# Start of the first feed-forward stage, place of the hidden low part, unrolled layers, half-block splits and rounded expert passes in a two-part transformer kernel

## The chip, the cores and the metric

The kernel runs as one program on one core of a Trainium2 chip. A core has five engines that each work through a queue of their own: TensorE (PE, matrix products; PEld is its weight load), VectorE (DVE), ScalarE (ACT), GpSimd (POOL) and SyncE (SP). They wait for each other through semaphores. The metric is the device time in microseconds (us); the profile shows one execution.

## What is computed

256 tokens of width 1024 pass two layers and then a hybrid layer with a mixture of experts:

```python
for l in range(DEPTH):                       # 2 layers
    mod = silu(c) @ w_ada[l] + b_ada[l]      # 9 rows of 1024: shift, scale, gate of three stages
    x = x + 0.5 * g1 * swiglu(modulate(x, sh1, sc1), ffn1_gate, ffn1_up, ffn1_down)   # 2816 wide
    x = x + g2 * token_mix(modulate(x, sh2, sc2), ...)                                # attention and merge
    x = x + 0.5 * g3 * swiglu(modulate(x, sh3, sc3), ffn2_gate, ffn2_up, ffn2_down)
x = rms_norm(x) * final_norm
x = x + gate1 * mix(modulate_2(x, ...))      # convolution and forgetting attention
h2 = modulate_2(x, ...)
x = x + gate2 * sum over experts e of comb[e] * swiglu_e(h2)    # 32 experts in 4 groups, width 256
```

All is float32. `comb` picks for each token one group of eight experts by softmax of `h2 @ w_rg + b_rg`, and in it the two best experts by `h2 @ w_re + b_re`.

## The kernel before

**Split products.** A float32 product is made of three products in the rounded type fp32r: each factor is split into a high part (the value rounded, by a copy on ScalarE) and a low part (the value less the high part, by a subtraction on VectorE), and `mm3` (L1542 to L1546) adds hi*hi, lo*hi and hi*lo in PSUM. A product with plain float32 operands is possible too and is used for small things: transposes with `ident`, the gathering of tokens, the spreading of results.

**The weight stream.** The weights come as units of 6144 columns (128 rows), each of three blocks of 2048 columns (1 MB). SP loads a block into one of three places of `raw` (`load_stream`), ScalarE makes `w_hi` (`split`, L466; L473 in the experts), VectorE makes `w_lo` (L854, L860), and TensorE waits for the block in `need`. Semaphores: `landed` for a load, `hi_done` and `split_done` count blocks, `used[j]` says that TensorE is through with block j of a unit. A feed-forward unit is 256 of the 2816 hidden columns: blocks 0 and 1 hold gate and up weights (k-chunks 0 to 3 and 4 to 7 of 512 columns), block 2 the down weights. An expert is one unit.

**Modulation.** `w_ada` comes in pairs of two columns of 128 values (1 MB a pair). VectorE multiplies each with silu(c) and sums (`ada_pair`, L877; `first_pair`, L1118), two instructions of 1024 columns a pair. POOL loads pairs into two slots of `ada_w` beside the layers (L441), each when `ada_done` says that the slot's former pair is used. The eight pairs of the very first shift and scale come ahead, loaded by SP into five places (`first_w`).

**A norm.** ScalarE sums squares (L482), VectorE scales (`norm_tile`, L898), TensorE turns the tokens (`norm`, L1581), both engines apply shift and scale (L499, L907) into `uTf`, ScalarE rounds it to `uT_hi` (L505), VectorE makes `uT_lo` (L912). TensorE keeps itself busy with zero products meanwhile (`keep_warm`, L1534).

**The start.** SP asks for c, pairs 0 and 1, x, all constants, the vectors, then pairs 2 to 7 with the blocks of unit 0 between them. VectorE does pairs 0 to 3 with the splits of blocks 0 and 1 between, pair 4, the norm of tile 0, pairs 5 to 7, the modulation (two instructions over all columns), and inside the layer loop the norm of tile 1. Then `gate_up` of unit 0 runs, all k of tile 0 first, then of tile 1.

**A feed-forward stage** (`ffn`, four times). In each pass of its loop TensorE turns the hidden values of unit i-1 (`turn`, L1610), does `gate_up(i)` and then `down(i-1)`. ScalarE does silu (L517, L519), VectorE `hidden` (L920), ScalarE the high part of the turned values (L523), VectorE the low part (`h_split`, L924). On VectorE the first unit has this order: split of block 0 of unit 1, pair 0 of the gate, `hidden(0)`, splits of block 1 of unit 1 and block 2 of unit 0, pairs 1 to 3 of the gate, the gate itself (L891, L893). Then the loop over i begins: `h_split(i-1)`, a pair (in ffn1), split of block 0 of unit i+1, a second pair (in ffn1), `hidden(i)`, split of block 1 of unit i+1, split of block 2 of unit i. In ffn2 a pass has one pair, from i = 2 on. Loops over i and the loop over the two layers are hardware loops (`Fori`) on PE, ACT, DVE and POOL.

**Routing.** After the last norm (`norm(n6 + 1, n6 + 2)`) TensorE makes the logits (48 products of 36 columns) in PSUM, VectorE adds the bias (L1409), ranks groups and experts, and makes `pick`, a 0/1 matrix for each of four groups that says which token stands at which of its 128 places (L1440). TensorE gathers the tokens of a group by plain float32 products with `pick` (`gather`, L2012: 16 products of 128 columns a group). Order on TensorE: gather 0, turned picks (L2020), gather 1, expert weights (L2026), gate/up of expert 0, gathers 2 and 3, and on. An expert is 24 products for gate and up and 12 for down, in 128 columns of places. After a group ScalarE copies the result (L798) and `spread` (L2066) puts it back to the tokens by four plain float32 products of 512 columns.

## Time and profile before

| | us |
|---|---|
| median of 3 runs | 2011.21 |
| lowest and highest run | 2007.62, 2019.69 |
| the profiled execution | 2009.42 |
| its span, first to last instruction | 2007.8 |

| engine | busy us | share of the span |
|---|---|---|
| PE | 1840.3 | 92% |
| PEld | 1492.2 | 74% |
| DVE | 1350.6 | 67% |
| ACT | 924.7 | 46% |
| POOL | 46.9 | 2% |

The mean granted TensorE clock was 0.940 of full. The stages follow each other: start to 58 us, ffn1 to 256, attention and merge to 496, ffn2 to 715, layer 1 the same to 1399, hybrid layer to 1664, routing to 1698, experts to 1985, end. A row of the timeline gives an instruction's start and length, and in square brackets how long the engine stood idle before it and which instruction released it. "issue" as releaser means that the engine waited for nothing that the profile shows. A group's busy time says nothing of whether it lies on the path; the idle times of TensorE do. A plain float32 product has two records in a count (x8 is four products).

### The profile page before, as it was taken

Reading aid. Unit: us, or ns where it says so; the run is one execution under the profiler, and the core shown is the slowest. Engines: PE = TensorE matmul, PEld = TensorE weight load, DVE = VectorE, ACT = ScalarE, POOL = GpSimd, SP = SyncE. Lnnn points to the kernel's source line nnn. Section 1 sums busy time; section 2 is a strip of 40 time slices with the busy share of each in tenths; the row PEclk is TensorE's granted clock in tenths of the full one; section 3 lists DMA queues with packets and bytes.
Section 4 is the critical chain, followed back from the end, with each engine's and each line's share of the span. In section 5 each row is a group of like instructions: output and inputs, shape, how many; then the busy total and the mean of one; then the engine's idle time right before and its main releaser. Section 6 shows DMA issues by size and latency. Waiting matters only on the chain.

```text
span 2007.8 us, 25016 instructions
## 1 busy us (share of the span) xinstructions
PE 1840.3 (92%) x8870; PEld 1492.2 (74%) x8870; DVE 1350.6 (67%) x1773; ACT 924.7 (46%) x1122; POOL 46.9 (2%) x92
## 2 busy tenths in 40 slices
PE   3799999999799988999999988998997998999997
PEld 2688777787588857886788767886876677878875
DVE  6777755856666557776557566665677275988885
ACT  2344453654444343444436552444433234777664
POOL 0000000000000000000000000000000000000000
PEclk6899998999899989999989998999999597999999
DMA  9788731324666648884412346665586051899993
GB/s 383 262 314 311 290 135 58 113 96 149 228 238 248 247 151 329 309 310 170 155 64 87 124 153 245 250 251 199 209 307 238 0 176 58 334 343 371 345 342 124
DMA packets 61361, 437.52 MB, mean 218 GB/s; under 512 B 6752, under 2 KB 7136, under 8 KB 9056
## 3 DMA queue, kind: packets, MB, share of 16 engines
q1 hardware_dynamic: 47056, 339.29, 45.6%
q0 software_dynamic: 12672, 92.28, 12.3%
q10 hardware_dynamic: 1552, 4.89, 0.7%
q8 instruction: 49, 0.80, 0.2%
q14 instruction: 32, 0.26, 0.0%
HBM read 435.38 MB, written 1.05 MB: 217 GB/s over the span
## 4 chain that ended last, share of the span: by engine, by line
PE 77%; DVE 12%; issue 4%; ACT 4%; DMA 3%; SPq 0%; DVEq 0%; ACTq 0%; POOL 0%; POOLq 0%
PE bank L1544 22%; PE bank L1545 21%; PE bank L1546 21%; DVE w_lo L854 3%; DMA ada_w<-ada_pairs 2%; DVE ada_w L877 2%; PE bank L1739 2%; ACT w_hi L466 1%; PE bank L1756 1%; DMA raw<-weight_stream 1%; PE bank L1610 1%; PE bank L1717 1%; PE bank L1713 1%; PE bank L1719 1%; PE bank L1534 1%
## 5 line engine op out<-in xcount | busy, mean ns | idle before, releaser
L854 DVE TENSOR_TENSOR w_lo<-raw,w_hi 128x2048 fp32r<-128x2048 f32 x214 | 489.5, 2291 | 330.9 <-ACT w_hi L466 330.5
L466 ACT ACTIVATE w_hi<-raw 128x2048 fp32r<-128x2048 f32 x214 | 408.7, 1913 | 462.9 <-PE bank L1546 462.9
L1544 PE MATMUL bank<-w_hi,uT_hi 128*128 128x512 f32 (+3 forms) x1456 | 564.3, 388 | 17.2 <-DVE w_lo L854 6.1
L1545 PE MATMUL bank<-w_lo,uT_hi 128*128 128x512 f32 (+3 forms) x1456 | 551.2, 379 | 0.0
L1546 PE MATMUL bank<-w_hi,uT_lo 128*128 128x512 f32 (+3 forms) x1456 | 549.6, 378 | 0.0
L1544 PE MATMUL bank<-w_hi,r_arena 128*128 128x512 f32 (+1 forms) x744 | 305.8, 411 | 36.6 <-DVE r_arena L924 31.6
L1544 PEld LDWEIGHTS bank<-w_hi,uT_hi 128*128 128x128 f32 x1456 | 278.3, 191 | 74.9 <-issue 12.7
L1546 PEld LDWEIGHTS bank<-w_hi,uT_lo 128*128 128x128 f32 x1456 | 277.8, 191 | 51.3
L1545 PEld LDWEIGHTS bank<-w_lo,uT_hi 128*128 128x128 f32 x1456 | 278.2, 191 | 47.9 <-issue 1.4
L1545 PE MATMUL bank<-w_lo,r_arena 128*128 128x512 f32 (+1 forms) x744 | 300.3, 404 | 0.0
L1546 PE MATMUL bank<-w_hi,r_arena 128*128 128x512 f32 (+1 forms) x744 | 297.9, 400 | 0.0
L877 DVE CUSTOM_DVE_ANT_0 ada_w<-ada_w,cmpw 128x1024 f32<-128x1024 f32 x176 | 207.2, 1220 | 30.4 <-DMA ada_w<-ada_pairs 30.4
L1544 PEld LDWEIGHTS bank<-w_hi,r_arena 128*128 128x128 f32 x744 | 146.2, 197 | 71.3 <-issue 35.3
L1546 PEld LDWEIGHTS bank<-w_hi,r_arena 128*128 128x128 f32 x744 | 145.7, 196 | 32.1
L1545 PEld LDWEIGHTS bank<-w_lo,r_arena 128*128 128x128 f32 x744 | 146.3, 197 | 28.1
L860 DVE TENSOR_TENSOR w_lo<-raw,w_hi 128x2048 fp32r<-128x2048 f32 x48 | 109.9, 2292 | 17.9 <-ACT w_hi L473 17.7
L473 ACT ACTIVATE w_hi<-raw 128x2048 fp32r<-128x2048 f32 x48 | 91.9, 1917 | 18.6 <-PE bank L1546 18.6
L860 DVE TENSOR_TENSOR w_lo<-ada_w,w_hi 128x2048 fp32r<-128x2048 f32 x32 | 73.3, 2292 | 20.0 <-ACT w_hi L473 18.9
L441 POOL DMA_DIRECT2D ada_w<-ada_pairs x88 | 46.7, 530 | 1477.7 <-DVE mods_gate L877 803.0
L473 ACT ACTIVATE w_hi<-ada_w 128x2048 fp32r<-128x2048 f32 x32 | 61.2, 1916 | 20.2 <-PE bank L1546 20.2
L517 ACT ACTIVATE arena<-bank 128x256 f32<-128x256 f32 x44 | 16.9, 384 | 115.0 <-PE bank L1546 115.0
L1581 PE MATMUL bank<-cst,arena 128*128 128x128 f32 x128 | 21.4, 324 | 46.4 <-DVE arena L898 46.4
(299 smaller groups left out, 1582.0 us busy)
## 6 DMA issues: line engine op xcount, KB each, us to landing
raw<-weight_stream SPq DMA_DIRECT2D x216, 1024.0 KB, 4.8
ada_w<-ada_pairs POOLq DMA_DIRECT2D x88, 1024.0 KB, 5.1
raw<-expert_blocks SPq DMA_DIRECT2D x48, 1024.0 KB, 4.8
ada_w<-expert_blocks SPq DMA_DIRECT2D x32, 1024.0 KB, 4.8
cmpw<-expert_blocks SPq DMA_DIRECT2D x16, 1024.0 KB, 4.7
arena<-ada_pairs SPq DMA_DIRECT2D x5, 1024.0 KB, 20.1
ada_w<-ada_pairs SPq DMA_DIRECT2D x3, 1024.0 KB, 15.0
cmpw<-compress_w ACTq DMA_DIRECT2D x2, 1024.0 KB, 5.4
```

What stands on the lines that cost most here:

```text
L441: pool.dma_start(ada_w[:, slot], ada[g]).then_inc(ada_landed[slot], 16)
L466: act.activation(w_hi[:, j * BLK:(j + 1) * BLK], raw[:, r * BLK:(r + 1) * BLK], ACT.Copy).then_inc(hi_done, 1)
L473: act.activation(w_hi[:, j * BLK:(j + 1) * BLK], place, ACT.Copy).then_inc(hi_done, 1)
L854: V.tensor_tensor(w_lo[:, b], raw[:, r * BLK:(r + 1) * BLK], f32(w_hi[:, b]), ALU.subtract).then_inc(split_done, 1)
L860: V.tensor_tensor(w_lo[:, b], place, f32(w_hi[:, b]), ALU.subtract).then_inc(split_done, 1)
L877: e = V.tensor_tensor_reduce(w[:, i], w[:, i], c, 1.0, 0.0, ALU.mult, ALU.add, dst[:, i:i + 1])
L1534: pe.matmul(dst, zeros[:, 0:P], zeros[:, 0:dst.shape[1]], start=True, stop=True, skip_group_check=True)
L1544: pe.matmul(dst, xh, w_hi[:, off:off + n], start=first, stop=False, skip_group_check=True)
L1545: pe.matmul(dst, xh, w_lo[:, off:off + n], start=False, stop=False, skip_group_check=True)
L1546: return pe.matmul(dst, xl, w_hi[:, off:off + n], start=False, stop=last, skip_group_check=True)
L1581: m = pe.transpose(ACC[b][:, (k % 2) * S + t * P:(k % 2) * S + (t + 1) * P], xn[:, t, k * P:(k + 1) * P], ident)
L1739: m = pe.matmul(HT[:, a * DH:(a + 1) * DH], pT[j % 2][:, kt, a], v, start=kt == 0, stop=kt == qt, skip_group_check=True)
```

## The change

1. **Start.** SP asks for x and the first 256 columns of the constants first, then the pairs in the order 0, 4, 1, 5, 2, 6, 3, 7 (a shift pair, then its scale pair), with the blocks of unit 0 after the second and fourth. VectorE does both norm tiles first, then for each couple b: a pair, the low part of couple b-1, a pair, the modulation of these columns, and for b < 2 the split of block b. ScalarE makes all of `uTf` and `uT_hi` couple by couple. TensorE runs `first_gate_up`, k outside and tile inside, with 8 zero products and a wait for the couple ahead of each second k.
2. **Hidden low part.** `h_split(f0)` stands on VectorE right behind the split of block 2 of unit 0, ahead of the gate's pairs 1 to 3, and in the loop at the end of a pass.
3. **Half blocks.** Each block split is two instructions of 1024 columns on ScalarE and on VectorE, each with its own count, and `need` waits for the half that it reads.
4. **Layers.** The loop over the two layers is a Python loop on all four engines.
5. **Routing and experts.** Logits are made turned (24 products, 36 rows by 256 columns), get their bias on ScalarE and are turned back. `xn` and the expert results are split into high and low parts, picks are fp32r, and one gather of 32 products of 512 columns serves all four groups. Picks are turned and expert weights gathered beside gate/up of expert 0. `spread` is eight fp32r products.

```diff
+        def halves(j, place):
+            return [(slice(j * BLK + i * HALF_BLK, j * BLK + (i + 1) * HALF_BLK), place[..., i * HALF_BLK:(i + 1) * HALF_BLK])
+                    for i in range(HALVES)]
...
+        FIRST_ORDER = (0, 4, 1, 5, 2, 6, 3, 7)
...
-            with act.Fori(0, DEPTH) as l:
+            for l in range(DEPTH):
...
             def split(u, js, order=IN_LINE):
                 for j in js:
-                    b, r = slice(j * BLK, (j + 1) * BLK), (order[j] + 3) % 3
-                    dve.wait_ge(hi_done, u * 3 + order[j] + 1)
-                    V.tensor_tensor(w_lo[:, b], raw[:, r * BLK:(r + 1) * BLK], f32(w_hi[:, b]), ALU.subtract).then_inc(split_done, 1)
+                    r = (order[j] + 3) % 3
+                    for i, (b, v) in enumerate(halves(j, raw[:, r * BLK:(r + 1) * BLK])):
+                        dve.wait_ge(hi_done, (u * 3 + order[j]) * HALVES + i + 1)
+                        V.tensor_tensor(w_lo[:, b], v, f32(w_hi[:, b]), ALU.subtract).then_inc(split_done, 1)
...
                 split(u0, (2,), LAST_BEHIND)
+                h_split(f0)
                 for j in (1, 2, 3):
                     ada_pair(pair_place(l, "gate1", j), mods_gate[:, 2 * j:2 * j + 2])
...
                 with dve.Fori(1, n - 1) as i:
                     places = pair_place(l, "ffn1", i)
-                    h_split(f0 + i - 1)
...
                     split(u0 + i, (2,), LAST_BEHIND)
-
-                h_split(f0 + n - 2)
+                    h_split(f0 + i)
+
...
+            for b in range(4):
+                first_pair(2 * b)
+                if b:
+                    first_lo(b - 1)
+                first_pair(2 * b + 1)
+                first_modulation(b)
+                if b < 2:
+                    first_split(b)
+            first_lo(3)
...
+            for t in range(T):
+                dve.wait_ge(xn_hi_done, t + 1)
+                V.tensor_tensor(xn_lo[:, t], xn[:, t], f32(xn_hi[:, t]), ALU.subtract).then_inc(xn_ready, 1)
...
+            def first_gate_up():
+                seen = set()
+                for k in range(KD):
+                    if k % 2 == 0:
+                        keep_warm(8, SPARE[:, 0:512])
+                        pe.wait_ge(uT_ready, k // 2 + 1)
+                    need(0, seen, k * 512, 512, IN_LINE)
+                    for t in range(T):
+                        m = mm3(GU[t][:, :], uT_hi[:, k, tok(t)], uT_lo[:, k, tok(t)], k * 512, 512, k == 0, k == KD - 1)
...
+            def gather(tiles):
 
                 for k in range(KD):
+                    dst = bank[GATHER_BANKS[k]][:, 0:tiles * P]
                     for t in range(T):
+                        for v in (xn_hi, xn_lo):
+                            m = pe.matmul(dst, v[:, t, k * P:(k + 1) * P], pick[:, t, 0:tiles], start=t == 0 and v is xn_hi,
+                                          stop=t == T - 1 and v is xn_lo, skip_group_check=True)
+                    m.then_inc(us_psum, 1)
...
+                for h in range(2):
+                    pe.wait_ge(ys_ready, 2 * n + h + 1)
+                    for t in range(T):
+                        for v in (y_hi, y_lo):
+                            m = pe.matmul(SPREAD[2 * t + h][:, :], pick_T[:, i, tok(t)], v[:, h * 512:(h + 1) * 512],
+                                          start=first and v is y_hi, stop=last and v is y_lo, skip_group_check=True)
```

## Rows read from the trace of the kernel before

**Rows 1.** Stretches: length, busy us by engine, TensorE clock, DMA share, GB/s

```profile
0.00:58.00 58.00, 25.40 (x97) 16.25 (x98) 31.48 (x54) 17.06 (x22) 1.47 (x6) 0.71 0.84 337
58.00:256.00 198.00, 184.20 (x797) 149.55 (x796) 150.40 (x195) 77.05 (x71) 12.67 (x24) 0.96 0.81 302
496.00:715.00 219.00, 203.14 (x892) 162.42 (x891) 136.61 (x154) 91.27 (x89) 6.33 (x12) 0.97 0.63 230
1698.00:1985.00 287.00, 286.88 (x1300) 231.26 (x1299) 242.01 (x170) 205.88 (x180) 0.00 (x0) 1.00 0.85 322
```

**Rows 2.** Groups by line: count, busy us, mean ns of one, idle before and releasers

```profile
L854 DVE TENSOR_TENSOR w_lo<-raw,w_hi 128x2048 fp32r<-128x2048 f32 x214 | 489.5, 2291 | 330.9 <-ACT w_hi L466 330.5
L466 ACT ACTIVATE w_hi<-raw 128x2048 fp32r<-128x2048 f32 x214 | 408.7, 1913 | 462.9 <-PE bank L1546 462.9
L941 DVE TENSOR_TENSOR x<-x,arena 128x1024 f32<-128x1024 f32 x16 | 19.6, 1226 | 0.6
L482 ACT ACTIVATE arena<-x 128x1024 f32<-128x1024 f32 x18 | 18.9, 1051 | 41.5 <-DVE x L941 41.5
L877 DVE CUSTOM_DVE_ANT_0 ada_w<-ada_w,cmpw 128x1024 f32<-128x1024 f32 x176 | 207.2, 1220 | 30.4 <-DMA ada_w<-ada_pairs 30.4
```

**Rows 3.** Chain that ended last, in time: start us, us, what; full and half clock

```profile
47.52 0.23 PE bank L1544
83.14 0.43 PE bank L1546
```

**Rows 4.** Timeline of TensorE: start us, us, instruction, count, idle before and releaser

```profile
46.47 0.58 PE L1544 MATMUL bank<-w_hi,uT_hi 128*128 128x512 f32 x1
...
62.30 1.11 PE L1610 MATMUL bank<-cst,arena 128*128 128x128 f32 x4 [3.69 <-DVE arena L920]
81.93 0.79 PE L1544 MATMUL bank<-w_hi,r_arena 128*128 128x512 f32 x1 [6.54 <-DVE r_arena L924]
...
541.99 0.79 PE L1544 MATMUL bank<-w_hi,r_arena 128*128 128x512 f32 x1 [6.57 <-DVE r_arena L924]
549.82 0.60 PE L1610 MATMUL bank<-cst,arena 128*128 128x128 f32 x4
```

**Rows 5.** Timeline of VectorE in the first feed-forward units of both stages, layer 0

```profile
76.78 1.22 DVE L877 CUSTOM_DVE_ANT_0 ada_w<-ada_w,cmpw 128x1024 f32<-128x1024 f32 x1 [5.55 <-DMA ada_w<-ada_pairs]
88.48 0.75 DVE L920 TENSOR_TENSOR arena<-arena,bank 128x256 f32<-128x256 f32 x2
...
541.16 0.68 DVE L924 TENSOR_TENSOR r_arena<-bank,r_arena 128x512 fp32r<-128x512 f32 x1
543.96 0.75 DVE L920 TENSOR_TENSOR arena<-arena,bank 128x256 f32<-128x256 f32 x2
```

**Rows 6.** Timeline of TensorE at further waits, and one stretch's clock

```profile
245.24 0.66 PE L1610 MATMUL bank<-cst,arena 128*128 128x128 f32 x4 [2.08 <-DVE arena L920]
...
509.21 0.49 PE L1544 MATMUL bank<-w_hi,uT_hi 128*128 128x512 f32 x1 [1.39 <-DVE w_lo L854]
...
1476.36 0.50 PE L1544 MATMUL bank<-w_hi,uT_hi 128*128 128x512 f32 x1 [1.81 <-DVE w_lo L854]
...
247.00:253.00 6.00, 5.62 (x13) 4.47 (x14) 2.57 (x3) 2.81 (x3) 0.00 (x0) 0.50 0.81 255
```

**Rows 7.** Timeline of VectorE at the change from layer 0 to layer 1

```profile
719.97 0.15 DVE L866 TENSOR_SCALAR stat<-stat 128x1 f32<-128x1 f32 x1 [2.29 <-issue]
```

**Rows 8.** Timeline of VectorE (first row) and TensorE in routing, experts and end

```profile
1679.81 0.23 DVE L1409 TENSOR_TENSOR arena<-bank,vec 128x72 f32<-128x72 f32 x1 [4.00 <-PE bank L1546]
...
1684.72 6.48 PE L2012 MATMUL bank<-arena 128*128 128x128 f32 x32 [0.91 <-DVE arena L1440]
...
1716.38 0.51 PE L1544 MATMUL bank<-w_hi,r_arena 128*128 128x512 f32 x1
...
1784.35 3.60 PE L2066 MATMUL bank<-arena 128*128 128x512 f32 x8
...
1989.84 0.51 PE L1544 MATMUL bank<-w_hi,r_arena 128*128 128x512 f32 x1 [4.50 <-DVE r_arena L1468]
```

341 lines of the change are left out of this document (190 added, 151 removed).

## The prediction

> **What bounds the kernel now.** I read the views in this order: the stretches by stage, the groups by line, then every place where TensorE waits. In the feed-forward loops [rows 1] TensorE is busy 184 of 198 us, and in the expert stretch 286.9 of 287 us at full clock, while VectorE has 150 of 198 and 242 of 287 us. So inside the loops TensorE sets the pace and work saved on other engines is worth nothing there. A 512-column product takes 0.23 us at the full clock (2.4 GHz) and 0.43 us at the half clock (1.2 GHz) [rows 3]; a feed-forward unit has 72 of them, an expert 36. The time that can be won lies in TensorE's waits and in the stretches at the half clock behind them: the start (58 us with 25 us of TensorE work, mean clock 0.71 [rows 1]), the first unit of each of four feed-forward stages [rows 4, 5], their ends and the joints [rows 6, 7], and the routing, group changes and end of the expert stage [rows 8]. A duration of one block split is 2.29 us on VectorE and 1.91 us on ScalarE [rows 2].
>
> **Part 1, the start.** Before, the first gate/up starts at 46.47 us [rows 4], after all eight modulation pairs, both block splits and both norms; 48 products of 0.23 us end it near 57.6. After, pairs come as (shift, scale) couples and TensorE gets two of eight k-chunks per couple. VectorE's queue sets the pace. The transfers ahead of the second pair are some 3.9 MB, at the stage's 337 GB/s [rows 1] about 12 us. Behind that stand on VectorE: eight pairs of 2 x 1.14 us (1.22 less the overlap [rows 2]) = 18.3; four half splits of about 1.15 = 4.6; three low parts of 512 columns, about 0.65 each by the rate of L941 [rows 2], = 2.0; four small modulation couples, an estimate of 0.35 each, = 1.4; two waits for ScalarE's evacuations, high part and first half split, estimated at 2.8 each by the rate of L482 (256+256+512+1024 columns), = 5.6; the last such wait without a split, 1.6, and the last low part, 0.7. Sum 46.2 us; the last 12 products end at about 49.5 us. The three other k-couples are dearer than they look, as each starts cold and has 8 warming products ahead, but they hide in the 6 to 11 us between couples. All at the half clock they would not: 4 x (12 + 8) x 0.43 us = 34 us from about 25 us on gives 59 us, no gain; that is the low bound. The gain here is 8 us.
> The next wait is that for `hidden` (62.30 us, 3.69 us long [rows 4]); pair 0 of the gate now waits for its own transfer, issued when the eighth pair is done (43.6 us), and the turn comes at about 53.5: 8.8 us earlier.
>
> **Part 2, the low part of h, out from behind three pairs and the gate.** VectorE's order in the loop stays the same for i >= 1 (last in an iteration instead of first in the next), so only the first unit changes, four times. There TensorE waits 6.54 and 6.57 us [rows 4] for L924 in two of them, and the code of the other two is the same. After, down(0) starts at once behind gate/up(1). But then turn(f1) is late next: it needs `hidden(f1)`, which stays behind the pairs, the gate and the split of the next block 0.
> - FFN2: hidden(f1) runs at 543.96 to 544.6 [rows 5], 0.6 us earlier without L924 ahead of it. TensorE turned at 549.82 [rows 4]. So 5.8 us is won, less what the new idle of some 4 us costs in clock: the products after 541.99 ran 4.3 us at 0.43 instead of 0.23 us [rows 3], a loss of about 2, which was partly there before too. 3.9 us each, 7.8 for two (bounds 2 x 2.5 and 2 x 5.9).
> - FFN1: hidden(f1) is also behind two pairs of the loop and ends at 89.2 us [rows 5], just when TensorE turns anyway. The stall of 6.5 us only moves from down(0) to turn(f1). The half clock, which before fell on down(0) inside that same wait for `hidden`, now falls behind it: 4 us at half speed, 2 us lost, against 0.8 us from half blocks. In layer 0 that takes 2 from the 8.8 us (6.8 left), in layer 1 it costs 1.2. The transfer that VectorE waits for (5.55 us at 76.78 [rows 5]) stays on this path, since its slot is freed by the pair before and not by h.
>
> **Part 3, half blocks.** 310 block splits become 620 per engine. Cost on VectorE: 2 x 1.226 against 2.291 us alone, +0.16 [rows 2]; back to back less, as ends overlap: +0.09. On ScalarE 2 x 1.051 against 1.913, +0.19 at most. In an expert of 36 x 0.23 + 0.2 = 8.5 us VectorE has 7.3 to 7.5 us (242 us over some 33 units [rows 1]), after 7.6 to 8.0: still under TensorE, so no cost. In FFN1 it has 12.8 of 16.9 us. The Trainium skill (VectorE: DVE Perf Modes, the section on the TRN2 errata) speaks against this part: many small operations each pay the fixed latency that one large one pays once, by its formula 1.22 us for 1024 columns against 2.29 us for 2048. The trace agrees (1.226 and 2.291), and by the page's +0.16 the chains below would lose some 1 us more in all than by +0.09.
> Gain: where a chain goes ScalarE, VectorE, TensorE with nothing in between, VectorE starts after half of 1.91 us, and TensorE after half of the 2.29 us. TensorE waits for w_lo 1.39 us (509.21; layer 1 has the same code) and 1.81 us (1476.36, one of two alike) [rows 6]; of each of the four about 1.1 to 1.25 goes: 4.6. The two attention joints and three merges, where the split stands ahead of the step waited for, give 0.7 to 0.85 each, of which I count half: 1.9. Together 6.5 (bounds 0 and 10).
> At the two FFN1 ends hidden waits behind such a chain: of the 2.08 us (245.24 [rows 6]) 0.75 goes, twice 1.5. The clock then was 0.50 over 247 to 253 us [rows 6]; if the shorter idle keeps it up, 24 products win 2.8 us more each. I give that 4 in 10: 2.2. Together 3.7.
>
> **Part 4, unrolled layers.** At the one layer change VectorE stood 2.29 us with issue as releaser [rows 7], its loop's jump, and TensorE's norm waited for it. That goes: 2.2 us (bounds 0 and 3). A page says the same: the Trainium skill (Runtime: NRT & Kernel Launch, Instruction fetch mechanics) holds that a taken branch out of the fetched pages stalls and straight code is streamed; the sum by it is the same 2.2.
>
> **Part 5, routing and experts.** Before, logits are added at 1679.81 us [rows 8]. After, 24 products of 256 columns replace 48 of 36, but ScalarE and VectorE first split xn and both blocks: VectorE is busy until about 1677.5. 2.3 us won. All eight picks must now be made before the gather (+1.2 us). The gather is 32 products of 512 columns; the old one ran 6.48 us at the half clock first [rows 8]; so 14 of the new at 0.43 and 18 at 0.23 = 10.1 us, ending near 1693.9 us, and gate/up starts 1.7 us behind, at 1695.6. Evacuations, expert weights and turned picks then go beside gate/up; hT's split, behind three split blocks' halves and two tiles' high and low parts on ScalarE and VectorE, is done near 1711.8 us, where down(0) started at 1716.38 [rows 8]. 4.6 us (bounds -2, if the gather stays at the half clock: 32 x 0.43 = 13.7, and 7). A spread took 3.60 us at 1784.35 [rows 8]; as 8 products of 0.23 it takes 1.8: 1.6 x 3 = 4.8, as VectorE's new low part of y (two of 0.69) is done about when gate/up ends. At the end the wait of 4.50 us (1989.84 [rows 8]) loses 0.8 to halves and the spread's first half some 0.5: 1.3. Together 10.7.
>
> **Sum.** 6.8 + 7.8 - 1.2 + 6.5 + 3.7 + 2.2 + 10.7 = 36.5 us. The profiled execution took 2009.4 us, 1.8 under the median of 2011.2; I take the sum from the median: 1975 us.
>
> **Rivals.**
> 1. The stalls only move: the start stays paced by warming products at the half clock (2 to 3 us won, not 8), FFN2 wins 2.5 each, the routing nothing. For it: clock 0.71 in the start, and FFN1, where the stall does move. Against: the six or more us between couples. Sum 36.5 - 6 - 3 - 5 - 4 = 18.5 us won or less: 1993 to 2005 us. Chance 0.16.
> 2. Clock and chains go well: FFN1 ends keep the full clock, start 11 us, FFN2 5.9 each, routing 7: 52 us won, about 1959 us. Chance 0.16.
> 3. Slower: half splits make VectorE the bound of the experts. From 7.4 us it decides from +0.37 us a block on; ScalarE and VectorE in lockstep, half by half, with a wait between each, would have to cost 1 us a block to give 10.4 us per expert, 32 x 1.9 = 61 us lost against 36.5 won: about 2036 us. No row has such a wait (the fixed part of a split is 0.16). Chance 0.04.
> 4. The forecast, 1966 to 1992: 0.64.
>
> A measurement of this kernel tells 1% (20 us, the runs of before lie 2007.6 to 2019.7) from no change. Faster by over 1% is all below 1991: cases 2, nearly all of 4: 0.80. Within 1%: most of case 1 and an edge of 4: 0.16. Slower 0.04. Range with 8 in 10: 1957 to 1994, between case 2 and the near end of case 1.
>
> **What would show it.** Right: first turn near 53 us and f1's near 81; no wait for L924 in the first units, but one of 7 us (FFN1) and 4 us (FFN2) for `hidden`; the 2.3 us issue gap gone; experts still 8.5 us each with VectorE above 90%; down(0) of the experts 15 us behind the gather's end or less. Wrong: half clock from 25 to 50 us, waits of TensorE for w_lo within the loops, a gather over 13 us.

## The result and the profile after

The changed kernel takes 1955.14 us (median of 4 runs, 1950.62 to 1964.89) against 2011.10; the ratio is 0.9722 with a 95% interval of 0.9673 to 0.9771. That is 56 us, where I forecast 36.5, and 1.9 us under the low end of the range. The profiled execution took 1957.13 us, its span is 1955.5.

TensorE's wait time and its busy time both fell. Of the 52.3 us of span, 24.3 are idle time (167.5 to 143.2 us) and 28.0 are busy time (1840.3 to 1812.3). Part 1 of the page of after (busy us, share, instructions):

```profile
PE 1812.3 (93%) x8756; PEld 1462.4 (75%) x8772; DVE 1375.6 (70%) x2086; ACT 953.6 (49%) x1427; POOL 47.1 (2%) x92
```

Its stretches, the answer to [rows 1] (length, busy us by engine, granted clock, DMA share, GB/s):

```profile
0.00:49.00 49.00, 30.26 (x117) 17.66 (x119) 31.71 (x60) 20.60 (x32) 1.39 (x6) 0.90 0.91 368
49.00:249.00 200.00, 184.42 (x808) 148.01 (x809) 154.38 (x232) 81.13 (x105) 12.77 (x24) 0.97 0.81 307
484.00:692.00 208.00, 199.02 (x877) 159.42 (x878) 136.22 (x186) 91.98 (x120) 6.38 (x12) 0.98 0.66 242
```

Groups by line (count, busy us, mean ns of one, idle before), the answer to [rows 2]: a half split costs 1221 ns on VectorE and 1053 ns on ScalarE. In all VectorE is busy 25 us longer, 504.0 for 489.5 us in this line.

```profile
L886 DVE TENSOR_TENSOR w_lo<-raw,w_hi 128x1024 fp32r<-128x1024 f32 x428 | 504.0, 1221 | 258.1 <-ACT w_hi L485 257.1 <-issue 0.3
L485 ACT ACTIVATE w_hi<-raw 128x1024 fp32r<-128x1024 f32 x428 | 428.7, 1053 | 419.1 <-PE bank L1611 413.9 <-DMA raw<-weight_stream 4.6 <-issue 0.5
```

TensorE's timeline of after (start, duration, instruction, idle before and releaser), the answer to [rows 4, 6, 8]:

```profile
24.36 0.80 PE L1609 MATMUL bank<-w_hi,uT_hi 128*128 128x512 f32 x1 [7.33 <-DVE uT_lo L1173]
34.87 0.50 PE L1609 MATMUL bank<-w_hi,uT_hi 128*128 128x512 f32 x1 [3.30 <-DVE uT_lo L1173]
...
51.61 0.65 PE L1689 MATMUL bank<-cst,arena 128*128 128x128 f32 x4 [2.40 <-DVE arena L954]
78.71 1.11 PE L1689 MATMUL bank<-cst,arena 128*128 128x128 f32 x4 [9.91 <-DVE arena L954]
...
237.08 0.66 PE L1689 MATMUL bank<-cst,arena 128*128 128x128 f32 x4 [1.26 <-DVE arena L954]
...
249.02 1.06 PE L1646 MATMUL bank<-cst,arena 128*128 128x128 f32 x8 [0.55 <-DVE arena L931]
...
507.07 0.71 PE L1689 MATMUL bank<-cst,arena 128*128 128x128 f32 x4 [2.96 <-DVE arena L954]
527.27 0.66 PE L1689 MATMUL bank<-cst,arena 128*128 128x128 f32 x4 [1.44 <-DVE arena L954]
...
1639.59 0.79 PE L2106 MATMUL bank<-picks,xn_hi 128*128 128x512 f32 x1 [2.09 <-DVE picks L1498]
1650.97 0.47 PE L1609 MATMUL bank<-w_hi,r_arena 128*128 128x512 f32 x1 [1.60 <-DVE r_arena L1458]
1666.96 0.50 PE L1609 MATMUL bank<-w_hi,r_arena 128*128 128x512 f32 x1 [1.15 <-DVE r_arena L1526]
1937.55 0.67 PE L1609 MATMUL bank<-w_hi,r_arena 128*128 128x512 f32 x1 [3.72 <-DVE r_arena L1526]
```

Where the time went, by the same instruction of TensorE in both timelines. "Turn" is the first transpose of `turn`, "norm" that of the next norm. "Idle" and "busy" say how much of what was won is idle time of TensorE and how much is busy time. The last column says what I had forecast.

| stretch | before ends at | after ends at | won in it | idle | busy | forecast |
|---|---|---|---|---|---|---|
| start, to first turn | 62.30 | 51.61 | 10.7 | 15.2 | -4.5 | 8.8 |
| ffn1 of layer 0, to its norm | 259.80 | 249.02 | 0.1 | -2.6 | 2.7 | -0.2 |
| attention and merge, to the turn of ffn2 | 522.25 | 507.07 | 4.4 | 1.6 | 2.8 | 1.8 |
| ffn2, to its norm | 717.72 | 696.16 | 6.4 | 5.0 | 1.3 | 3.9 |
| layer change, second tile of the norm | 721.40 | 697.53 | 2.3 | 2.3 | 0.0 | 2.2 |
| first gate/up of layer 1, to its turn | 741.98 | 716.27 | 1.8 | 0.4 | 1.5 | 0 |
| ffn1 of layer 1, to its norm | 939.20 | 911.25 | 2.2 | 1.3 | 1.0 | 0.6 |
| attention and merge, to the turn of ffn2 | 1205.14 | 1172.02 | 5.2 | 1.8 | 3.3 | 1.8 |
| ffn2, to its norm | 1405.51 | 1364.60 | 7.8 | 4.7 | 3.1 | 3.9 |
| hybrid layer, to its last norm | 1663.75 | 1619.98 | 2.9 | 2.8 | 0.1 | 2.9 |
| routing, experts, end | 2007.8 | 1955.5 | 8.5 | -8.0 | 16.6 | 10.7 |

From the first turn to the last norm (the nine rows between the first and the last) both kernels run the same products, so busy time won there is clock: 15.9 us busy and 17.2 us idle, 33.1 in all, for 16.9 forecast. (The trace of after lacks some ten records of products there; at 0.23 us each they are worth 2 us at most.) In the first and the last row the instructions themselves differ: the start has new products on zeros, the routing and the spreads are other products.

### The profile page after: what moved, and what is told of

Its sections match the earlier page's. It is cut to its first block, busy times and chain, and to the rows that moved or that the text cites. A ratio compares the mean times of both kernels' runs of the same rounds, so it can differ in the third digit from the quotient of the medians.

```text
span 1955.5 us, 25172 instructions
## 1 busy us (share of the span) xinstructions
PE 1812.3 (93%) x8756; PEld 1462.4 (75%) x8772; DVE 1375.6 (70%) x2086; ACT 953.6 (49%) x1427; POOL 47.1 (2%) x92
## 3 DMA queue, kind: packets, MB, share of 16 engines
q0 software_dynamic: 12672, 92.28, 12.8%
## 4 chain that ended last, share of the span: by engine, by line
PE 77%; DVE 14%; ACT 4%; DMA 3%; issue 3%; POOL 0%; ACTq 0%; DVEq 0%; SPq 0%; POOLq 0%
PE bank L1609 22%; PE bank L1610 22%; PE bank L1611 22%; DVE w_lo L886 3%; DMA ada_w<-ada_pairs 2%; DVE ada_w L910 2%; PE bank L1819 2%; PE bank L1836 1%; PE bank L1689 1%; ACT w_hi L485 1%; PE bank L1797 1%; PE bank L1793 1%; PE bank L1799 1%; DVE arena L972 1%; DVE w_lo L893 1%
## 5 line engine op out<-in xcount | busy, mean ns | idle before, releaser
L886 DVE TENSOR_TENSOR w_lo<-raw,w_hi 128x1024 fp32r<-128x1024 f32 x428 | 504.0, 1221 | 258.1 <-ACT w_hi L485 257.1
L485 ACT ACTIVATE w_hi<-raw 128x1024 fp32r<-128x1024 f32 x428 | 428.7, 1053 | 419.1 <-PE bank L1611 413.9
L1609 PEld LDWEIGHTS bank<-w_hi,uT_hi 128*128 128x128 f32 x1440 | 274.4, 191 | 81.6 <-DVE uT_lo L1173 13.5
L1609 PE MATMUL bank<-w_hi,r_arena 128*128 128x512 f32 (+1 forms) x744 | 301.8, 406 | 13.5 <-DVE r_arena L958 5.7
L1609 PEld LDWEIGHTS bank<-w_hi,r_arena 128*128 128x128 f32 x744 | 143.3, 193 | 47.4 <-DVE r_arena L958 6.6
L1611 PEld LDWEIGHTS bank<-w_hi,r_arena 128*128 128x128 f32 x744 | 143.0, 192 | 33.1
L893 DVE TENSOR_TENSOR w_lo<-raw,w_hi 128x1024 fp32r<-128x1024 f32 x96 | 113.2, 1222 | 13.0 <-ACT w_hi L493 13.0
L493 ACT ACTIVATE w_hi<-raw 128x1024 fp32r<-128x1024 f32 x96 | 96.2, 1053 | 17.6 <-PE bank L1611 17.6
L893 DVE TENSOR_TENSOR w_lo<-ada_w,w_hi 128x1024 fp32r<-128x1024 f32 x64 | 75.3, 1221 | 9.6 <-ACT w_hi L493 8.7
L537 ACT ACTIVATE arena<-bank 128x256 f32<-128x256 f32 x44 | 16.9, 384 | 111.1 <-PE bank L1611 111.1
L493 ACT ACTIVATE w_hi<-ada_w 128x1024 fp32r<-128x1024 f32 x64 | 64.1, 1055 | 13.4 <-PE bank L1611 13.4
L1599 PE MATMUL bank<-zeros 128*128 128x512 bf16 (+1 forms) x236 | 56.9, 395 | 6.3 <-DMA cst<-shape_constants 5.8
```

The lines of the kernel that those rows point to most:

```text
L485: act.activation(w_hi[:, b], v, ACT.Copy).then_inc(hi_done, 1)
L493: act.activation(w_hi[:, b], v, ACT.Copy).then_inc(hi_done, 1)
L886: V.tensor_tensor(w_lo[:, b], v, f32(w_hi[:, b]), ALU.subtract).then_inc(split_done, 1)
L893: V.tensor_tensor(w_lo[:, b], v, f32(w_hi[:, b]), ALU.subtract).then_inc(split_done, 1)
L1599: pe.matmul(dst, zeros[:, 0:P], zeros[:, 0:dst.shape[1]], start=True, stop=True, skip_group_check=True)
L1609: pe.matmul(dst, xh, w_hi[:, off:off + n], start=first, stop=False, skip_group_check=True)
```

## The experiments

The times are medians, the ratios those to runs of the kernel before on the same chip. Its median was 2010.15 us beside the first four experiments of the table, 2008.54 beside the four from "before, warmed" to "start not paced", and 2005.38, 2011.60 and 2011.48 us beside the pairs that follow. Idle and busy are TensorE's, of the profiled execution. The ratio is not the quotient of the two medians: the two differ by up to 0.3% (0.9735 against 0.9766 for the quarter blocks), so a gain named here in microseconds of medians is good to some 6 us. Where a trace is read, it is one run, and not always a typical one: the traced runs of the three parts (1974.00 us), of the whole blocks (1990.84) and of the warmed kernel (2007.67) are the slowest or nearly the slowest of their kernels, that of the spread pairs (1946.60) is the fastest.

| kernel | us | ratio to before, 95% | span | busy | idle |
|---|---|---|---|---|---|
| before | 2011.10 beside the change | 1 | 2007.8 | 1840.3 | 167.5 |
| change | 1955.14 | 0.9722 [0.9673, 0.9771] | 1955.5 | 1812.3 | 143.2 |
| half blocks alone | 1984.46 | 0.9851 [0.9824, 0.9878] | 1983.2 | 1824.6 | 158.6 |
| low part of h alone | 2008.77 | 0.9996 [0.9976, 1.0016] | 2004.2 | 1838.9 | 165.3 |
| layers unrolled alone | 1995.77 | 0.9907 [0.9878, 0.9937] | 1994.8 | 1831.7 | 163.1 |
| these three | 1962.30 | 0.9733 [0.9698, 0.9769] | 1972.3 | 1828.1 | 144.2 |
| before, warmed | 2000.27 | 0.9958 [0.9934, 0.9982] | 2006.0 | 1845.6 | 160.4 |
| change, hidden(f1) first | 1951.26 | 0.9713 [0.9693, 0.9733] | 1948.9 | 1807.0 | 141.9 |
| change, whole blocks | 1981.48 | 0.9854 [0.9825, 0.9884] | 1989.0 | 1837.2 | 151.8 |
| change, start not paced | 1972.99 | 0.9817 [0.9796, 0.9838] | 1976.9 | 1817.9 | 159.0 |
| change, pairs spread | 1953.80 | 0.9739 [0.9701, 0.9777] | 1944.9 | 1806.4 | 138.5 |
| change, quarter blocks | 1958.54 | 0.9735 [0.9695, 0.9776] | 1958.5 | 1820.8 | 137.7 |
| pairs spread, apart | 1955.81 | 0.9725 [0.9677, 0.9773] | 1962.2 | 1820.8 | 141.4 |
| the same, ends warmed | 1954.25 | 0.9727 [0.9687, 0.9768] | 1955.8 | 1820.5 | 135.3 |
| before, warmed more | 2006.47 | 0.9970 [0.9950, 0.9990] | 2006.6 | 1849.5 | 157.1 |
| best combination | 1947.22 | 0.9670 [0.9632, 0.9709] | 1945.6 | 1812.4 | 133.2 |

### Which part won it: each of three parts alone, and the three

The edits are those of the change, one part at a time: the half blocks (part 3), the place of `h_split` (part 2), the layer loops (part 4).

> The kernel before with half blocks alone. The changed kernel as a whole wins 14.6 us in the attention and merge stretches, where I had counted 6.5. Theory: that is the half blocks' doing; then this kernel wins about 15 us in those stretches and 1.5 to 5 us at the two ends of the first feed-forward stages, together 16 to 20 us (about 1993 us), its start and first units stay as before, within 1 us, and its expert loops too. Rival: the half blocks give 6.5 to 8 us as forecast, and the rest of the 14.6 us came from steps that another part put ahead: about 2003 us.

> The kernel before with the low part of h moved and nothing else. Theory: each second feed-forward stage wins 5.5 to 6.5 us and none of it is lost to the clock again; in each first one the 6.5 us wait moves from the first down product to turn(f1) and nothing is won, or up to 2 us lost: together 9 to 13 us (about 2000 us). Rival, as I forecast: 3.9 us in each second stage because the clock falls behind the new wait, 2 us lost in each first one: together 4 us (2007 us).

> The kernel before with the two layers written out and nothing else. Theory: only the layer change moves; the 2.29 us that VectorE stood with issue as releaser go, and with the shorter idle the clock rises earlier in the next stage: 2 to 4 us (2008 us). Rival: the straight code is twice as long and must be loaded in other places, with new issue gaps there: no gain, or up to 3 us lost.

> Half blocks, the moved low part of h and the written out layers together, with the old start and the old routing. The changed kernel won 56 us, 10.7 of it before the first turn and about 8.5 from the routing on. Theory: the parts do not help each other and this kernel wins the rest, 35 to 38 us (about 1975 us), close to the sum of the three single kernels. Rival: the shorter waits together keep the clock up where one alone does not; then this kernel wins over 5 us more than the sum of the three.

**Half blocks** won 25.7 us, more than the theory's 16 to 20. TensorE's instructions are the same ones, so its two times can be compared. Idle fell by 8.9 us, close to what I had forecast for this part (6.5, and 1.5 at the ends). Busy fell by 15.7 us for the same products: that is the clock. It shows best from the second tile of a norm to the first transposes behind the projections, in layer 0 and 1 (length, busy us by engine, granted clock, DMA share, GB/s). Before:

```profile
261.27:343.40 82.13, 77.51 (x489) 66.14 (x489) 39.25 (x68) 33.99 (x50) 0.00 (x0) 0.92 0.30 103
940.66:1026.16 85.50, 80.73 (x488) 69.12 (x489) 39.23 (x68) 33.98 (x50) 0.00 (x0) 0.88 0.28 99
```

With half blocks alone:

```profile
259.14:338.46 79.32, 74.77 (x488) 64.65 (x489) 40.06 (x76) 34.75 (x58) 0.00 (x0) 0.96 0.30 107
931.78:1011.07 79.29, 74.76 (x489) 64.64 (x489) 40.06 (x76) 34.75 (x58) 0.00 (x0) 0.96 0.30 107
```

Idle time is length less the first busy number: 4.6 and 4.8 us before, 4.6 and 4.5 with half blocks. The stretch waits as long as before and is still 2.8 and 6.2 us shorter, as the clock is 0.96 instead of 0.92 and 0.88. What did change is how the waiting is cut: the wait ahead of the compressed keys is 1.74 us instead of 2.53. That the shorter wait does it is likely and not sure. In the 18 such stretches of the nine kernels with the wait of 1.74 us the stretch took 77.8 to 84.9 us, 80.6 in the mean; in the eight with the longer wait, 80.8 to 87.2, 85.5 in the mean. The means lie 4.9 us apart for 0.8 us of wait, but the two groups overlap.

**The low part of h** alone is no change in the median. Its trace shows why. In the second stages TensorE no longer stands 6.57 us in front of down(0), but 4.12 us in front of turn(f1), and the unit behind that wait runs 19.4 us instead of 16.9: from turn(f0) to turn(f2) 42.14 us instead of 44.42. In the first stages it is 44.39 instead of 44.00. So this part alone follows my forecast's mechanism (the stall moves, the clock takes part of the gain), at 2.3 us for my 3.9.

**Unrolling** won 14.4 us, where I had 2.2. The 2.29 us at the layer change are gone and idle fell by 4.4 us, but busy fell by 8.6 for the same products. The rest of the idle lies in the first units: VectorE's wait for the transfer of the gate's last pair was 4.45, 4.58, 4.56 and 3.57 us in the four stages, before 5.55, 5.67, 5.51 and 4.93. By positions 1.1 us came at the end of the first stage, 1.4 in the attention of layer 0, and 5.2 from the last turn of layer 0 to the first of layer 1. Then the attention of layer 1 lost 3.1 us to the clock and later stretches won 6: a good part of this size is the clock's.

**The three together** won 47.8 us, over the theory's 35 to 38 and 6.4 us over the sum of the single ones, 41.5. That is the rival's side, but it is not shown by the times: by the ratios the surplus is 4 us, and the interval of the ratio is 7 us wide to either side. The traces show one place where two parts help one another, the second stages. There VectorE stands for the transfer of the gate's last pair, ahead of `hidden(f1)`. Its timeline before, with the low part of h alone, with the three, and in the change:

```profile
536.86 1.23 DVE L877 CUSTOM_DVE_ANT_0 ada_w<-ada_w,cmpw 128x1024 f32<-128x1024 f32 x1 [5.67 <-DMA ada_w<-ada_pairs]
...
544.32 1.23 DVE L877 CUSTOM_DVE_ANT_0 ada_w<-ada_w,cmpw 128x1024 f32<-128x1024 f32 x1 [5.96 <-DMA ada_w<-ada_pairs]
...
527.45 1.23 DVE L887 CUSTOM_DVE_ANT_0 ada_w<-ada_w,cmpw 128x1024 f32<-128x1024 f32 x1 [3.74 <-DMA ada_w<-ada_pairs]
...
520.01 1.23 DVE L910 CUSTOM_DVE_ANT_0 ada_w<-ada_w,cmpw 128x1024 f32<-128x1024 f32 x1 [3.28 <-DMA ada_w<-ada_pairs]
```

That wait, TensorE's wait ahead of turn(f1) and what the next unit took (16.9 to 17.0 us at full clock), in the second stages of both layers:

| kernel | VectorE's wait for the transfer, us | wait ahead of turn(f1), us | the next unit, us |
|---|---|---|---|
| low part of h alone | 5.96, 5.17 | 4.12, 3.35 | 19.35, 19.66 |
| the three | 3.74, 3.80 | 2.00, 2.05 | 18.50, 18.54 |
| change, whole blocks | 4.76, 3.10 | 2.71, 1.02 | 18.30, 17.02 |
| change | 3.28, 3.01 | 1.44, 1.14 | 17.00, 17.00 |

TensorE's wait is VectorE's less 1.7 to 2.1 us. What goes with the shorter transfer wait is the unrolling: in the ten second stages of the kernels that keep the loop over the layers it is 4.65 to 5.96 us, in the twelve of those that write the layers out and leave VectorE's order in the stage as in the change or before, 2.99 to 4.76. Why the pair lands earlier there is not shown. Half blocks do not set it (1.02 us with whole ones in layer 1). The unit behind took 17.0 us in six cases with a wait of 1.02 to 1.53 us (change, whole blocks, quarter blocks, start not paced) and 18.3 to 19.7 in six with 2.00 to 4.12. That is why the stage won 6.4 us and not 3.9: some 2 us of transfer wait went, and the clock stayed up behind what was left. The granted clock of that unit, first with the three, then in the change (columns as above):

```profile
534.71:553.21 18.50, 18.50 (x77) 15.11 (x78) 13.01 (x16) 5.38 (x8) 0.53 (x1) 0.91 0.81 290
```

```profile
527.27:544.27 17.00, 17.00 (x76) 13.97 (x77) 12.94 (x16) 5.95 (x8) 0.53 (x1) 1.00 0.91 320
```

### The change with whole blocks, and with quarter blocks

```diff
-HALVES, HALF_BLK = 2, BLK // 2
+HALVES, HALF_BLK = 1, BLK
```

The kernel with quarter blocks has `HALVES, HALF_BLK = 4, BLK // 4` there.

> The changed kernel with whole blocks. Theory: the half blocks are worth here what they were alone, about 9 us of waits and 10 to 16 us of clock: 1975 to 1981 us, with TensorE's busy time up by 10 us or more. Rival: the other parts already hold the clock up, so the half blocks are worth only their waits: 1963 to 1967 us.

> The changed kernel with quarter blocks of 512 columns. Theory: the fixed part of a split, 0.15 us from whole to half blocks, comes twice more, so that an expert's three blocks cost VectorE about 1 us more; it had some 7.9 of 8.5 us, so it becomes the bound by 0.3 to 0.5 us per expert, 32 experts: 10 to 16 us lost in the expert stretch, 2 or 3 us won at the joints: 1963 to 1970 us. Rival: the fixed parts overlap enough that TensorE stays the bound, and the shorter chains win: 1950 to 1955 us.

Whole blocks cost 26.3 us (1981.48 against 1955.14), as much as half blocks won alone; the theory holds. Both traces have the same 8756 products: idle rose by 8.6 us and busy by 24.9, in one of the slower runs of this kernel. Quarter blocks change nothing (1958.54), and the theory of a VectorE bound falls. The stretch from the first expert's down to the last one's is 270.31 us long, 270.59 in the change, though VectorE is busy for 93% of the time. The group by line, then a stretch of the experts (columns as above):

```profile
L886 DVE TENSOR_TENSOR w_lo<-raw,w_hi 128x512 fp32r<-128x512 f32 x856 | 532.8, 685 | 218.9 <-ACT w_hi L485 215.7
```

```profile
1671.00:1945.00 274.00, 270.57 (x1196) 218.11 (x1197) 253.47 (x434) 218.85 (x433) 0.00 (x0) 0.99 0.87 328
```

Back to back the ends overlap: a block costs 2.29 us whole, 2.36 in halves and 2.49 in quarters (busy time by number of blocks, 214 each), so an expert's three blocks cost 0.4 us more in quarters than in halves, not 1. The Trainium skill (VectorE: DVE Perf Modes, the section on the TRN2 errata) has a fixed latency for each instruction; the trace agrees for one alone (2291, 1221, 685 ns), but back to back only some 0.07 us of it is paid.

### Is it the clock? The kernel before with its waits filled

```diff
                 turn(f0 + n - 1)
+                keep_warm(5, GU[0][:, :])
                 down(u0 + n - 1, f0 + n - 1, last=True)
...
+                keep_warm(9, SPARE[:, 64:512])
                 pe.wait_ge(cqT_ready, l * 3 + 2)
```

> The kernel before, with idle time filled and none removed: 9 products on zeros ahead of the 2.53 us wait in front of the compressed keys (twice), and 5 ahead of the last down product of each feed-forward stage, in front of its 1.49 us wait. Each wait ends when it did before. Theory: what the half blocks won beyond the waits they shorten (15.7 of 24.6 us were TensorE's busy time for the same products) is the granted clock; then the fillers alone hold it up, 3 to 6 us per attention stretch and up to 3 us at an end, 6 to 14 us in all (about 2000 us). Rival: the clock only follows the real work, or the busy time came from something else; then nothing is won (2010 us), or the fillers' own time is lost, up to 2 us.

Won: 8.3 us, with no wait ended earlier. At the ends the theory holds. From the last turn to the norm the four feed-forward stages take 12.8, 11.8, 13.0 and 17.2 us where they took 14.6, 13.4, 14.4 and 18.8, so 1.4 to 1.8 us each. The span of this trace is only 1.8 us under before's all the same, so most of these 6.4 us were lost again elsewhere in that run; the 8.3 us are the median of ten runs that lie between 1987.25 and 2009.02. At the joint ahead of the compressed keys it does not hold: both stretches took 85.5 us, the longer of the two lengths before, at a clock of 0.88, although the wait was down from 2.53 to 0.71 us. The clock fell 8 us behind it, among small products. So I filled those too:

```diff
-                keep_warm(16, SPARE[:, 64:512])
+                keep_warm(22, SPARE[:, 64:512])
...
+                    if j % 2:
+                        keep_warm(1, SPARE[:, 64:512])
```

(and one behind every second pair of the 15-column products).

> The warmed kernel (the kernel before with fillers at the joint and at the ends), with fillers also among the small products behind the joint: 6 more before the 1.68 us wait, one of 448 columns behind every second of the 16 products of 60 columns, one behind every second pair of 15-column products. They cost about 3 us per layer at full clock. From the last norm product to the first transposes of the next part took 82.1 and 85.5 us before, 85.5 twice in the warmed kernel (half clock from 320 to 340 us, behind the small products), 79.3 at best. Theory: the clock falls there because the products are small, not because of the waits; then the fillers hold it at full and both stretches take 81 to 83 us, in all 1995 to 1998 us. Rival: the clock falls there with the fillers as well; the stretches take 87 us or more and the kernel 2002 to 2008 us.

Both stretches still took 85.6 us, between the two forecasts, and the kernel 2006.47, where the rival had it: nothing was won by them. The clock did fall, ten us later. Two windows of 2 us of each kernel, columns as above. Warmed:

```profile
318.00:320.00 2.00, 1.92 (x17) 1.93 (x17) 0.02 (x1) 0.00 (x0) 0.00 (x0) 0.92 0.00 0
320.00:322.00 2.00, 2.00 (x11) 2.00 (x11) 0.00 (x0) 0.00 (x0) 0.00 (x0) 0.50 0.00 0
```

Warmed more:

```profile
328.00:330.00 2.00, 2.00 (x15) 1.55 (x14) 0.00 (x0) 0.00 (x0) 0.00 (x0) 1.00 0.00 0
330.00:332.00 2.00, 2.00 (x9) 1.27 (x8) 0.00 (x0) 0.00 (x0) 0.00 (x0) 0.53 0.00 0
```

What decides there stays open. The unrolled kernel has the same waits in both layers (2.52 and 1.68 us) and 80.8 us in the one, 87.2 in the other. The Trainium skill (TensorE: Matmul & The Clock Gate, Part 1) says that the chip sets the clock by how busy the array has been, and that this watch runs freely and does not start with the kernel. Equal waits with unequal clocks fit that; no run here shows the watch itself.

The runs of one kernel say the same. Over 13 runs of the kernel before, the shortest has 2003.24 us at a mean clock of 0.941 and the longest 2017.15 at 0.934. A mean lower by 0.007 is 28 us more at half clock (0.007 x 2010 x 2), in which 14 us of work are lost, and 14 us lie between the two runs. Over all 13 runs time and mean clock go together (correlation -0.93), so most of the scatter goes with the clock. What starts a slower clock in one run and not in another, the times do not say.

### The start

```diff
             def first_gate_up():
                 seen = set()
+                pe.wait_ge(uT_ready, 4)
```

> The changed kernel, with TensorE waiting for all four couples before its first gate/up. Theory: the pacing is what wins the start: the last low part is ready near 45.1 us, 48 products follow, the first turn comes at 58 to 59 us instead of 51.6, and the span is 7 us longer, 1962 us. Rival: the start is won by the earlier transfers and norm, and warming products on the path eat the pacing: the first turn comes by 54 us.

The first turn comes at 67.37 us, not at 58 to 59, and the kernel is 17.9 us slower than the change. I had left two things out. The four groups of eight warming products are now on the path (1.6 us each at full clock, the first 3.0), and after 31.15 us of waiting the clock is 0.50 to 49 us and 0.76 to 54:

```profile
45.49 3.60 PE L1599 MATMUL bank<-zeros 128*128 128x512 bf16 x8 [31.15 <-DVE uT_lo L1173]
...
45.00:49.00 4.00, 3.51 (x9) 1.50 (x10) 0.43 (x1) 0.00 (x0) 0.00 (x0) 0.50 0.94 389
49.00:54.00 5.00, 4.93 (x18) 3.42 (x18) 0.00 (x0) 0.00 (x0) 0.00 (x0) 0.76 0.78 315
```

So the pacing is what wins the start, and it does so twice: the products are done while VectorE still works on pairs, and the last of them run at full speed. Its size is overstated here: of the 15.8 us between the two first turns some 7.8 (3.0 and three times 1.6) are the warming products, which a kernel that waits for all couples would not need; an estimate for the pacing alone is 8 us. No run leaves them out. The low bound of my forecast for the start, all at half clock, was not near.

### The wait that moved: VectorE's order in the first units

The change leaves 9.91 us ahead of turn(f1) in the first stage (6.19 in layer 1). Three orders were tried. First, `hidden(f0 + 1)` and the splits around it before pair 3 and the gate, with the first pass of the loop written out:

```diff
                 h_split(f0)
-                for j in (1, 2, 3):
+                for j in (1, 2):
                     ada_pair(pair_place(l, "gate1", j), mods_gate[:, 2 * j:2 * j + 2])
+                split(u0 + 2, (0,), LAST_BEHIND)
+                hidden(f0 + 1)
+                split(u0 + 2, (1,), LAST_BEHIND)
+                split(u0 + 1, (2,), LAST_BEHIND)
+                h_split(f0 + 1)
+                ada_pair(pair_place(l, "gate1", 3), mods_gate[:, 6:8])
...
-                with dve.Fori(1, n - 1) as i:
...
+                with dve.Fori(2, n - 1) as i:
```

> The changed kernel, with VectorE's first unit in another order: the next block 0 and hidden(f1) now stand ahead of the third modulation pair and the gate, and in the first stages ahead of the loop's two pairs too. Theory: the 9.91 and 6.19 us that TensorE waits for hidden ahead of turn(f1) in the first feed-forward stages are that queue; they fall to 2 to 4 us and the clock rises 2 us earlier, so 10 to 16 us are won (about 1942 us); the second stages win 0 to 2 us. Rival: VectorE waits for the pairs' transfers in any order, and the wait comes back at turn(f2) or at the loop's first pair: 0 to 4 us won.

Turn(f1) comes at 68.59 us with no wait, and 10.18 us are waited one unit later. The rival was right; 3.9 us are won in the median, by ratios whose intervals overlap (0.9713 and 0.9722). TensorE's timeline, then VectorE's, which stands for transfers:

```profile
95.89 1.12 PE L1702 MATMUL bank<-cst,arena 128*128 128x128 f32 x4 [10.18 <-DVE arena L954]
```

```profile
82.95 1.23 DVE L910 CUSTOM_DVE_ANT_0 ada_w<-ada_w,cmpw 128x1024 f32<-128x1024 f32 x1 [3.57 <-DMA ada_w<-ada_pairs]
...
88.22 1.23 DVE L910 CUSTOM_DVE_ANT_0 ada_w<-ada_w,cmpw 128x1024 f32<-128x1024 f32 x1 [2.69 <-DMA ada_w<-ada_pairs]
```

Second, all pairs behind `hidden` and `h_split` in every unit, pair 0 too, and the owed ones spread over later units (pairs per unit of a first stage: 1, 2, 1, 2, 3, 3, 2, 3, 2, 3 with the gate's four among them). This kernel and the next two also write VectorE's loop over the units out, so their gain is not that of the order alone:

> The changed kernel, with VectorE's feed-forward loops in a new order: in each unit hidden and the low part of h come before the modulation pairs, pair 0 of the gate goes behind hidden(f0), and the pairs that the first units owe are spread over the later ones, two or three to a unit. Theory: putting hidden(f1) first only pushed 10 us of owed pairs in front of turn(f2); VectorE has 4 us to spare in each of the first stages' units, so owed pairs are free once they are spread. Then the waits at turn(f0) (2.4 to 3.3 us, four times) fall to below 1 us and those at turn(f1) or turn(f2) (9.9 and 6.2 us) to below 2 us, the clock comes back earlier, and 15 to 25 us are won: 1930 to 1940 us. Rival: the pairs' transfers, one at a time for each of the two slots, are the bound and show as waits further on: 1945 to 1955 us.

Third, each third pair ahead of `hidden`, 8 us from the others; fourth, the same with 5 products on zeros at the ends:

> As the spread kernel, but in a first stage's units each third pair stands ahead of the block split and hidden, eight us from the other two, and the last unit of the loop has none. In the spread kernel the wins at the first turns (12 us at turn(f1)) were all given back in the same stage: 3.66 and 8.04 us of waits for hidden where VectorE stood 5.28 and 3.19 us for a pair's transfer, three pairs having come in a row on two slots. Theory: with the pairs apart those two waits go, and the two first stages keep 8 us or more of the 12: turn of the last unit near 229 us instead of 236.6, in all 1930 to 1940 us. Rival: the transfers (6.3 MB per unit, up to 371 GB/s wanted where the stage had 312) or VectorE's own 16 of 16.9 us are the limit, and the waits come in other units: 1945 to 1955 us.

> The kernel of the run before with 5 products on zeros ahead of the last down product of each feed-forward stage. In the warmed kernel before, each of the four ends was 1.4 to 1.8 us shorter by them. Theory: the same again where the clock falls at that end (13.5 us from the last turn to the norm), so 1.6 us at each of the second stage of layer 0 and whichever others fall: 2 to 6 us under the run before. Rival: those ends already keep the clock, within 1 us of the run before.

In the second stages the new order has what it promised: the turn of f0 waits 0.67 us instead of 2.96, no later one waits over 1 us, and from the merge's last norm to the last turn the stage takes 190.2 us in all three against 194.7. The wait of f0 and that of f1 are the order's doing; how much of the rest is the written-out loop, no run separates. In the first stages it wins 12 us at turn(f1) (66.74 us) and gives all of it back, as the rival said. TensorE's waits in the spread kernel, then what VectorE waited for in the third kernel between 50 and 240 us (us in total, times, longest):

```profile
156.26 1.12 PE L1679 MATMUL bank<-cst,arena 128*128 128x128 f32 x4 [3.66 <-DVE arena L954]
...
236.56 1.12 PE L1679 MATMUL bank<-cst,arena 128*128 128x128 f32 x4 [8.04 <-DVE arena L954]
```

```profile
DVE ada_w L910 <- DMA ada_w<-ada_pairs: 26.5, 5, 6.5
DVE w_lo L886 <- ACT w_hi L485: 17.6, 10, 3.8
```

With three pairs in a unit VectorE stands for their transfers in either order (in the change only 5.4 us in this window). The last turn came at 236.56, 242.14 and 241.01 us, in the change at 237.08: in these orders a first stage is held by its pairs. Whether the two slots or the rate of the transfers holds them, no run separates. Warming the ends of the third kernel gave 1.6 us in the median, within the scatter. The traces have the rival's case: all four ends take 11.95 and 17.2 us with and without the products on zeros, as they already kept the clock.

The best combination takes the spread order in the second stages, the first order in the first stages, and the 5 products at the ends of the second stages.

> The changed kernel with the second feed-forward stages of the spread kernel, the first stages of the kernel with hidden(f1) first, and 5 products on zeros at the ends of the second stages. Theory: in the second stages few pairs (1 MB each) are owed, so what the order wins stays won: 4.2 us each by the three spread kernels; with 1.6 us at an end where the clock fell (13.5 us) and about 1 us in each first stage, 10 to 13 us are won: 1942 to 1946 us. Rival: the wins of single stages sink in the clock's own scatter and are not there in the median: 1950 to 1955 us.

It took 1947.22 us, 8 us less than the change (0.9670 against 0.9722 of before); the intervals of the two ratios still overlap. The median is 1 us off the theory's 1942 to 1946. The second stages are 5.9 and 4.1 us shorter from the merge's last norm to the next one, the first stages 2.9 us shorter and 1.3 longer from first turn to norm.

## Why the prediction was off

**Right.** The bound was read rightly: inside the loops TensorE set the pace before and after, and the gain came where the forecast placed it. The stall of [rows 4] did move from down(0) to turn(f1), 9.91 and 6.19 us. The 2.29 us of [rows 7] went, and logits came 2.5 us earlier for my 2.3. Of that 1.2 us were gone at the gather, as worked out, and down(0) of the experts came 5.6 us earlier than the last norm had, forecast 4.6. The start gave 10.7 us for 8.8; the last low part was ready at 45.3 us for my 46.2 and the first turn came at 51.6 for 53.5.

**The step that failed: the clock's part of the gain.** My sum counted regained full clock in one place only, the ends of the first stages (2.2 us), and lost clock behind the new waits ahead of turn(f1) (2 us in each of four stages). Everywhere else I took idle time won as time won. Between the first turn and the last norm that makes 22.6 us of idle time less 5.6 of clock, about 17 in all. The runs showed 17.2 us of idle time and 15.9 of busy time for the same products, 33.1 in all: the clock term came out with the other sign and nearly as large as the idle time. Half blocks alone (8.9 us idle for my 8) got 15.7 us from it, unrolling (4.4 idle for 2.2) 8.6. Of the 19.5 us by which the forecast was low, 16.2 lie there, 1.9 in the start, and 2.2 go the other way from the routing on; the other 3.7 are the difference between the medians (56.0 us) and the traced runs (52.3).

**Mis-sized terms**, by the table above:
- Half blocks in the attention and merge stretches: 3.6 forecast, 9.6 measured in the whole change, of it 3.5 idle and 6.1 busy; the hybrid layer gave its 2.9. (The 14.6 us of the expectation took in parts of the neighbouring stretches.)
- FFN2: 3.9 each forecast (5.8 idle less 1.9 for the clock behind a new wait of 4 us), 6.4 and 7.8 measured (5.0 and 4.7 idle, 1.3 and 3.1 busy). I had `hidden(f1)` only 0.6 us earlier. It came some 2 us earlier, as VectorE's wait for the transfer of the gate's last pair shrank from 5.67 and 4.93 us to 3.28 and 3.01, and behind the 1.44 and 1.14 us that TensorE then waited the clock stayed up. I had seen such a wait in FFN1 [rows 5] and took it as fixed; here it was in no term of mine.
- FFN1's ends: I gave the full clock 4 chances in 10. It held at both: 11.9 us from turn to norm for 14.6 and 14.4. This term was 3.7 and came to 6.7. That it held at both was partly luck: with the same code there the end of layer 0 took 13.5 us in the traces with hidden(f1) first, with the start not paced and with quarter blocks, and the end of layer 1 11.95 in all three.
- FFN1 of layer 0: the stall did not only move, it grew from 6.54 to 9.91 us, where I had 7.
- The gate/up behind the layer change: 1.8 us more, 1.5 of it busy time, in no term.
- Spreads and the end: 6.1 forecast, 2.9 measured. The three inner group changes did win some 1.5 us each, near the forecast, and the last `hidden` wait 0.8. But an expert took 8.6 us in the first and the last group and 8.5 in the others, for 8.44 to 8.51 before and with the three parts alone. A feed-forward unit took 16.95 for 16.87 in the same way. So the change made the loops themselves a little longer, with its new start, routing or expert code and not with the half blocks; why is not shown. Behind the last down nothing was won, as the new low part of y stands ahead of the last spread (1.43 us).

Rival 2, all clock and chains well, at 1959 us with 0.16, was nearest to the case that came. Its figure was partly luck: its items come to 48.5 us, not 52 (36.5, 3.4 for the ends, 2.2 for the start, 4.0 for FFN2, 2.4 for the routing), which is 1963 us. It had the start, the ends and FFN2 about right and held nothing for the clock in the attention stretches. Rival 3 fell further than thought: not even quarter blocks bind VectorE.

## What to carry over

When TensorE is the bound, cost a removed wait twice: the wait, and the products behind it at half clock. In the kernel before, 0.06 of 2008 us of missing clock are 241 us at half speed, so up to 120 us lie there, as against 167 us of idle time. Cost parts that shorten the same wait together: in the second stages a wait of 2.0 us cost the unit behind it 1.5 us, one of 1.4 us nothing. Before a wait is taken as fixed, see what ends it: here it was a transfer, and another part of the change made it land earlier. A stall ahead of a queue that owes work (here 1 MB pairs on two slots) moves with every reordering until the owed transfers fit; where few are owed, the reordering stays won.

## What the runs showed of the hardware

- Two kernels with the same products and the same idle time in a stretch differ by up to 6.2 us in it by the granted clock (4.8 us idle and 85.50 us, 4.5 and 79.29).
- Products on zeros in a wait keep more of the full clock at the feed-forward ends (1.4 to 1.8 us won each where it fell, nothing where it had held), and do not in the compressed-key stretch, where the clock falls even with the waits filled to 0.71 us.
- Splitting a 2048-column VectorE instruction in two costs 0.07 us back to back, in four 0.20, where the instruction alone has 0.15 us beyond its columns.
- Writing the two passes of the layer loop out was worth 14.4 us in the median, six times the 2.29 us that VectorE stood at the jump. In the traces 4.4 us of the gain are idle time and 8.6 are clock; no loss to the longer program shows.
- In the second stages a wait of TensorE of 1.02 to 1.53 us left the next unit at 17.0 us (six cases), one of 2.00 to 4.12 us made it 18.3 to 19.7 (six cases).
